# A one-core decoder layer on Trainium2: router heads every four items, gate products between the k steps, 34 more rows in the first half

## The reference, cut to what matters

```python
qv = (tb @ wq).reshape(n, PEER_HEADS, 2, PEER_HALF)
s = jnp.einsum('thcd,hckd->thck', qv, sub_keys).astype(jnp.float32)
s_top, i_top = lax.top_k(s, PEER_TOPK)
cand = (s_top[:, :, 0, :, None] + s_top[:, :, 1, None, :]).reshape(n, PEER_HEADS, -1)
...
best, pos = lax.top_k(cand, PEER_TOPK)
idx = jnp.take_along_axis(cand_idx, pos, axis=-1)
g = jax.nn.softmax(best, axis=-1).astype(tb.dtype)
u = expert_u[idx]
act = jax.nn.gelu(jnp.einsum('td,thkd->thk', tb, u))
v = expert_v[idx]
return jnp.einsum('thk,thkd->td', g * act, v)
```

## Time and profile before

| | us |
|---|---|
| median of 3 runs | 1953.18 (1946.73 to 1957.24) |
| the profiled execution | 1952.73, of which the span 1950.6 |
| mixer, in that span | 0 to 470 |
| U half (items 0 to 143) | 470 to 1243 |
| V half (items 144 to 271) | 1243 to 1818 |
| closing | 1818 to 1951 |

### The profile page before, as it was taken

One profiled execution on the slowest core, in us unless ns is written; L12 is line 12 of the kernel. 1 busy time (PEld: TensorE's weight loads), 2 busy tenths in 40 slices (PEclk: granted clock), 3 DMA queues, 4 the chain that ended last, 5 costly groups with the idle time before them and its releaser, 6 DMA issues.

```text
span 1950.6 us, 29824 instructions
## 1 busy us (share of the span) xinstructions
PE 1828.0 (94%) x11502; PEld 1756.7 (90%) x11502; DVE 1461.8 (75%) x2584; ACT 848.7 (44%) x1236; POOL 514.0 (26%) x415
## 2 busy tenths in 40 slices
PE   6999989998999999999999999699999999999694
PEld 5999977788999999999999999699999999999693
DVE  4736587556478778999999998588888878788524
ACT  4556672314333333347777776233233323323322
POOL 1200120000000002345444444344445444344000
PEclk9999989998999999999999999899999999999897
DMA  3222333114334447789999999999999999897111
GB/s 128 78 67 85 114 123 99 50 55 166 119 126 157 152 159 237 242 314 343 377 360 351 369 360 354 379 386 359 361 383 379 381 377 359 336 372 264 66 54 46
DMA packets 162616, 462.63 MB, mean 237 GB/s; under 512 B 16496, under 2 KB 74544, under 8 KB 160048
## 3 DMA queue, kind: packets, MB, share of 16 engines
q1 hardware_dynamic: 116400, 292.99, 41.5%
q0 software_dynamic: 46080, 167.79, 23.0%
HBM read 405.46 MB, written 55.27 MB: 236 GB/s over the span
## 4 chain that ended last, share of the span: by engine, by line
PE 69%; DVE 13%; DMA 11%; ACT 3%; issue 2%; SPq 1%; POOL 0%; DVEq 0%; ACTq 0%; POOLq 0%
PE PS L449 11%; DMA Rw<-vn 8%; PE PS L1416 8%; PE PS L1417 8%; PE PS L1418 8%; PE PS L1429 5%; PE PS L1430 5%; PE PS L1431 5%; PE PS L1405 5%; PE PS L1476 4%; PE PS L1898 3%; DVE Hl L1789 2%; PE PS L129 2%; ACT Rh L164 1%; DVE Rl L169 1%
## 5 line engine op out<-in xcount | busy, mean ns | idle before, releaser
L169 DVE TENSOR_TENSOR Rl<-Rw,Rh 128x1024 fp32r<-128x1024 f32 x272 | 332.1, 1222 | 171.2 <-ACT Rh L164 167.7
L164 ACT CAST Rh<-Rw 128x1024 fp32r<-128x1024 f32 x272 | 284.2, 1046 | 389.8 <-PE PS L1431 341.1
L1386 POOL DMA_INDIRECT ug<-un,idxU x160 | 239.2, 1495 | 579.6 <-DVE dots L1797 354.3
L1429 PE MATMUL PS<-Hh,Rh 128*128 128x384 f32 x1024 | 352.2, 344 | 37.1 <-DVE Hl L1789 36.9
L1416 PE MATMUL PS<-Xh,Rh 128*128 128x384 f32 x1024 | 353.9, 346 | 3.8 <-DVE Rl L169 2.7
L1430 PE MATMUL PS<-Hl,Rh 128*128 128x384 f32 x1024 | 349.1, 341 | 0.0
L1431 PE MATMUL PS<-Hh,Rl 128*128 128x384 f32 x1024 | 348.8, 341 | 0.0
L1417 PE MATMUL PS<-Xl,Rh 128*128 128x384 f32 x1024 | 345.0, 337 | 0.0
L1418 PE MATMUL PS<-Xh,Rl 128*128 128x384 f32 x1024 | 344.0, 336 | 0.0
L1386 POOL DMA_INDIRECT ug<-vn,idxU x160 | 232.2, 1451 | 280.2 <-DVE yacc L1802 218.6
L1429 PEld LDWEIGHTS PS<-Hh,Rh 128*128 128x128 f32 x1024 | 194.7, 190 | 46.5 <-issue 46.3
(11 more groups left out here) (378 smaller groups left out, 3074.6 us busy)
## 6 DMA issues: line engine op xcount, KB each, us to landing
Rw<-uw SPq DMA_DIRECT2D x144, 512.0 KB, 4.8
Rw<-vn SPq DMA_DIRECT2D x128, 512.0 KB, 7.9
Wr<-wm SPq DMA_DIRECT2D x51, 512.0 KB, 3.2
acts<-Ab SPq DMA_DIRECT2D x128, 192.0 KB, 5.4
gates<-stg SPq DMA_DIRECT2D x12, 2048.0 KB, 9.8
Gq<-gates SPq DMA_DIRECT2D x16, 1536.0 KB, 12.9
Aq<-acts SPq DMA_DIRECT2D x32, 768.0 KB, 10.3
w_ple_ring<-w_ple SPq DMA_DIRECT2D x8, 640.0 KB, 4.3
```

Source lines behind the costliest of these rows:

```text
L164: a.copy(self.Rh[:, q, :], self.Rw[:, q, :]).then_inc(self.S("rhi"), 1)
L169: v.tensor_tensor(self.Rl[:, q, :], self.Rw[:, q, :], self.Rh[:, q, :].bitcast(F32), ALU.subtract).then_inc(self.S("rlo"), 1)
L1386: p.indirect_dma_start(out=ug[:, r % 4, :], out_offset=None, in_=un if r < IDC else vn, in_offset=bass.IndirectOffsetOnAxis(ap=idxU[:, r % ...
L1429: pe.matmul(out, Rh[:, q, w], hh, start=(g == 0), stop=False)
```

## The change

- **Router.** Heads begin every four items (0, 4, 8, 12, then 24, 28, 32, 36), so that the items 0 to 15 and 24 to 39 are Q, U, Q, U. The six parts of `topk` stand in the iterations n + 5, 5, 6, 7, 7, 8. Decoding begins at the iterations 21 and 45; the lookups of block 0 and of the samples are both in the next iteration, then comes `softmax` with `idx`, then one lookup in each of the three iterations 24 to 26 and 48 to 50; `sx` is counted up at the end of the last.
- **Gates.** TURN is 51 (was 77), G0 is 55 (79), GEND is 131 (139). The products stand between the k steps of a U item: with one unit in an item one product after each second k step, with two units one after each. The wait for a unit's inputs and for `gev` is at its first product. `one_hot_act` runs two items ahead, as the one-hot matrices on DVE did and do.
- **Rows.** 30 rows after item 53, 156 after item 131, 180 after item 143; 140 are left to the V half. The GELU of the dot products (`sparse_act`) can therefore now fall in the U half.
- **Mixer.** DVE adds the squares of the channels 0 to 6 into `sqa` (`square_add`, six additions of 128x544), and PE sums twice instead of eight times, at the end. SP issues the load of `ce` for chunk 1 first, and it has a semaphore of its own.

```diff
-HEAD_AT = [0, 6, 12, 18, 34, 40, 46, 52]
-LOOK = [29, 63]
+HEAD_AT = [0, 4, 8, 12, 24, 28, 32, 36]
+LOOK = [21, 45]
...
             if n == 38:
+                sp.wait_ge(S("act_c"), 2 * NXC)
+                sp.wait_ge(S("cout_s"), 2 * NXC)
+                spread_e(1)
                 sp.wait_ge(S("mm"), OL0)
...
-            if n >= OS0 + 2:
-                d = n - OS0 - 2
-                if d == 0:
-                    pe.wait_ge(S("root"), 3)
-                sums(3, d, sq[:, d % 2, :])
-        for d in range(ND - 2, ND):
-            sums(3, d, sq[:, d % 2, :])
+        pe.wait_ge(S("root"), 3)
+        pe.wait_ge(S("sqa"), ND - 2)
+        for q in range(2):
+            m = pe.matmul(pair(3)[:, q, :], ones[:, :], sqa[:, q * HT:(q + 1) * HT], start=True, stop=False)
+        pe.wait_ge(S("sq_ready"), 4 * ND)
...
+        def square_add(d):
+            v.wait_ge(S("sq_ready"), 3 * ND + d + 1)
+            if d >= 2:
+                v.wait_ge(S("sqa"), d - 1)
+            v.tensor_tensor(sqa[:, :], sq[:, 0, :] if d == 1 else sqa[:, :], sq[:, d % 2, :], ALU.add
+                            ).then_inc(S("sqa"), 1)
...
-    TURN = 77
-    G0 = 79
-    GEND = 139
+    TURN = 51
+    G0 = 55
+    GEND = 131
...
-    ROWS = [(46, 0), (78, 36), (VI - 1, 146), (NALL - 5, 2 * IDC)]
+    ROWS = [(25, 0), (53, 30), (GEND, 156), (VI - 1, 180), (NALL - 5, 2 * IDC)]
...
+            turn = [(j, u) for j in units(m) for u in range(4)]
             for k in range(ND):
...
-            r.then_inc(S("wmm"), 1)
+                if k == ND - 1:
+                    r.then_inc(S("wmm"), 1)
+                for j, u in turn[k * len(turn) // ND:(k + 1) * len(turn) // ND]:
+                    gate_product(j, u)
...
+        def gate_product(j, u):
+            if u == 0:
+                pe.wait_ge(S("ga"), j + 1)
+                pe.wait_ge(S("gaa"), 2 * j + 2)
+                pe.wait_ge(S("gb"), j // 2 + 1)
+                need(pe, "gev", j - 1)
...
-            for j in units(n + 1):
+            for j in units(n + 2):
                 one_hot_act(j)
...
-            for part in range(6):
-                if head_at(n, 5 + part) is not None:
-                    topk(head_at(n, 5 + part), part)
+            for part, at in enumerate((5, 5, 6, 7, 7, 8)):
+                if head_at(n, at) is not None:
+                    topk(head_at(n, at), part)
...
-                if 1 <= step < 9 and step % 2 == 1:
-                    lookup(g, step // 2)
-                if step == 8:
+                if step == 1:
+                    lookup(g, 0)
                     lookup(g, NDB)
-                if step == 9:
+                if step == 2:
                     softmax(g)
+                if 3 <= step < 6:
+                    lookup(g, step - 2)
+                if step == 5:
+                    v.wait_ge(tc, ntc[0])
+                    v.sem_inc(S("sx"), 1)
```

More of the change, by code:

```diff
@@ L246, in mixer @@
     rstdB = at("rstdB", A6 + 2 * T * 4, [P, T])
+    sqa = at("sqa", A6 + T * 4, [P, T])
     yh = at("yh", A4, [P, ND, T], F32R)
@@ L625, in tensor @@
                     sums(2, k, sq8[:, k, :])
-            if n >= OS0 + 2:
-                d = n - OS0 - 2
-                if d == 0:
-                    pe.wait_ge(S("root"), 3)
-                sums(3, d, sq[:, d % 2, :])
-        for d in range(ND - 2, ND):
-            sums(3, d, sq[:, d % 2, :])
+        pe.wait_ge(S("root"), 3)
[3 more added lines that the diff above has]
+        pe.wait_ge(S("sq_ready"), 4 * ND)
+        for q in range(2):
+            m = pe.matmul(pair(3)[:, q, :], ones[:, :], sq[:, (ND - 1) % 2, q * HT:(q + 1) * HT], start=False,
+                          stop=True)
+        m.then_inc(S("sq_free"), ND)
     def scalar(a):
@@ L1231, in vector @@
                 ssd_add(n - OS0 - 1)
+                if n >= OS0 + 4:
+                    square_add(n - OS0 - 3)
             if n == NW - 1:
@@ L1234, in vector @@
                     ring.lo(v, m)
+        square_add(ND - 2)
         ring.lo(v, 3)
@@ L1466, in turns @@
                 m.then_inc(S("gtp"), 1)
-        def gate_unit(j):
-            pe.wait_ge(S("ga"), j + 1)
-            pe.wait_ge(S("gaa"), 2 * j + 2)
-            pe.wait_ge(S("gb"), j // 2 + 1)
-            need(pe, "gev", j - 1)
-            for u in range(4):
-                t = 4 * (j % 2) + u
-                out = PS[:, 2 + j % 2, u * PK:(u + 1) * PK]
-                m = pe.matmul(out, Boh[:, (j // 2) % 2, t, :], Aoh[:, j % 4, u, :], start=True, stop=True)
-            m.then_inc(S("gmm"), 1)
+        def gate_product(j, u):
[4 more added lines that the diff above has]
+                need(pe, "gev", j - 1)
+            t = 4 * (j % 2) + u
+            m = pe.matmul(PS[:, 2 + j % 2, u * PK:(u + 1) * PK], Boh[:, (j // 2) % 2, t, :], Aoh[:, j % 4, u, :],
+                          start=True, stop=True)
+            if u == 3:
+                m.then_inc(S("gmm"), 1)
         for n in range(NIT):
@@ L1489, in tensor @@
                 turns()
-            for j in units(n):
-                gate_unit(j)
         pe.wait_ge(S("glu"), PK)
@@ L1556, in h_hi, with sparse_act @@
             a.copy(Hh[:, i % 2, :, :], Aq[:, i % 3, :, :]).then_inc(S("hhi"), 1)
+        def sparse_act(n):
+            if rows_upto(n) >= IDC > rows_upto(n - 1):
+                a.wait_ge(S("sdt"), IDC)
+                a.activation(coef[:, :], dots[:, :], ACT.Gelu_apprx_tanh).then_inc(S("cf"), 1)
         def exps(g):
@@ L1589, in scalar @@
                 gate_out(j)
+            sparse_act(n)
             if n == NIT - 1:
@@ L1597, in scalar @@
                 h_hi(g // 4 + 1)
-            if rows_upto(n) >= IDC > rows_upto(n - 1):
-                a.wait_ge(S("sdt"), IDC)
-                a.activation(coef[:, :], dots[:, :], ACT.Gelu_apprx_tanh).then_inc(S("cf"), 1)
+            sparse_act(n)
     def vector(v):
```

12 lines of the change are left out of this document (4 added, 8 removed).

## The result

| | median, us | lowest to highest | ratio to before (95% interval) |
|---|---|---|---|
| before | 1954.6 | 1946.7 to 1957.2 | |
| after | 2012.0 | 2010.7 to 2016.5 | 1.0305 (1.0275 to 1.0335) |

What follows compares the result with a forecast made beforehand. PE was taken to set the pace, with waits in places and DMA and DVE nearly full. From 1952.7 us: mixer -5, gate waits +44, clock +14, turn +28, U half's end +5, V half -21 gave 2017 us; 8-in-10 range 1980 to 2044.

Steps and rivals of the forecast that it cites:

- The gate wait: Gate items: PE waits 2.3 us for ACT's bank copy behind each of 19 two-unit items, +44 us.
- the first rival: Gate items: k steps are not held, or ACT copies in time; the gate term goes, 1960 us, chance 0.08.
- The clock behind these waits: Gate items: lower PE clock costs 1.5 us more behind half of the 19 waits, +14 us (0 to +28).
- The turn: Behind item 51: PE waits for the last lookup after DVE's burst in iterations 41 to 50, net +28 us.
- its sign: Behind item 51: one long PE wait at the transposes, 17 us or more.
- The end of the U half: Items 132 to 144: DMA must carry 27.3 MB, 73 us against 50.5 of PE; net +5 us (-8 to +15).
- The V half: V items: 34 fewer rows relieve DMA and remove waits, -21 us (-27 to -12).
- The rival by which the rows give nothing: V half gains nothing, as waits on `Hl`, not bandwidth, set it: 2038 us, chance 0.08.
- The mixer: Before item 0: fewer ones matmuls and an earlier `ce` load against a longer end, sum -5.1 us (-6.5 to -3).
- the five groups of ones matmuls: Mixer: six groups of ones matmuls of 0.92 us were to leave PE's chain, -5.5 us.
- the earlier `ce`: Mixer: load issued some 3 us sooner, removing DVE's wait, -1.05 us.
- the end: Mixer's end: two DVE additions before PE's first sums, then a reciprocal waiting for ACT's root, +1.45 us.

Runs made afterwards that it cites:

- experiment 1: Changed kernel with the gate products behind an item's 24 k-step matmuls again instead of between them: 1962.5 us, ratio 1.0048 to the kernel before.
- experiment 2: Changed kernel with ACT copying the gate bank directly behind the copy of the item's output, products still between the k steps: 1976.6 us, ratio 1.0123.
- experiment 6: Changed kernel with the 34 rows back in the V half (row 126 at item 131, 146 at the end of the U half): 2022.4 us, ratio 1.0371.
- Experiment 7: Changed kernel with SP's wait for the stored gates and the first V-half loads six items later, at item 137: 2013.3 us, ratio 1.0320.
- Experiment 4: Kernel of experiment 1 with the turn behind item 57 instead of 51 and gates from item 61 instead of 55: 1951.9 us, ratio 0.9995.
- Experiment 5: Kernel before with only the rows' part of the change (180 rows, not 146, by the end of the U half; `sparse_act` there): 2004.5 us, ratio 1.0274.
- experiment 3: Kernel before with only the mixer's part of the change: 1945.9 us, ratio 0.9956.
- experiment 8: Kernel of experiment 1 with a looser timetable: second decoding at item 51, turn behind 61, gates in 65 to 129, fewer early rows: 1931.2 us, ratio 0.9894.

## Why the prediction was right, point by point

- **The gate wait** (+44, measured 44.1). The forecast had the place (the item behind one of two units), the count (19) and the size (2.3; such an item is 7.41 where its work is 5.09, so 2.32 longer). Experiments 1 and 2 show the cause: the wait goes with the place of the products, and shrinks with ACT's order. The k steps behind a waiting product waited with it, so the first rival fell: the product of item 68 started at 873.21 and the next k step at 873.63. That agrees with what the Trainium skill (TensorE: Matmul & The Clock Gate, Step-by-step: what each phase is for) says, that matmuls stay in program order.
- **The clock behind these waits** (+14, measured 4.6). This term was mis-sized. I took half of 19 from two V items; three of 19 (the items 68, 88 and 112, 8.9 to 9.0 us) had it, at 1.5 each. Two instances were no base for a share. The price of one was right. In the profiles of experiments 6 and 7, with the same 19 waits, it was three of 19 again.
- **The turn** (+28, measured +27.5). Part of it fell due earlier than forecast: 14 us were lost in the items 45 to 50 to the ring's low parts, and the turn's own wait was then 15.4, under the 17 or more that the prediction named as its sign. Experiment 4 shows that a later turn alone recovers 11 us; what stays behind is spent waiting for DVE.
- **The end of the U half** (+5, measured +7.1; 75.0 us for 50.5 of work, so 24.5 late where 22.5 was forecast). Experiment 7 moves the loads and not the time, which speaks for the amount of work, not SP's blocking; experiment 6 takes 4 rows of 24 and 30 earlier ones away and gains 7.9.
- **The V half** (-21, measured -24.3). Experiments 5 and 6 put and take the rows alone: -23.1 and +19.4. The rival by which the rows give nothing has fallen. The size is less sure than it looks: the three profiles with 146 rows before it have 575.0, 570.2 and 568.4 us for this half, and before's is the longest. That the relief was DMA's is argued: ACT waited 46.2 us for weights to land in this half of before and 6.4 in after's, but the rows also took 41 us of DVE's work with them. The Trainium skill (DMA: Bandwidth & Descriptors, Measured) gives 425 GB/s for a long stream. Over this half the mixed stream here moved 352 GB/s before and 335 after.
- **The mixer** (-5, measured +0.3 in the profile). The term failed in that profile. It had four parts: the five groups of ones matmuls gave -4.4; the earlier `ce` -1.15, of which 0.4 was lost again at the next chunk; the end cost +3.1 and not +1.45, as the eight last matmuls ran at 0.46 instead of 0.23 us each behind PE's idle time; and +1.55 was the clock behind an unchanged wait. The rest, +0.7, is there from the first loads on. Over all profiles the mixer gives -1.9, and over the runs of experiment 3 the kernel gains 7.7.

That the sum came within 5 us is partly luck, as errors cancelled: the clock's 9 and the V half's 3 too much stood against the mixer's 5 and the end's 2 too little.

What the prediction hardly asked is what the 34 rows cost in the U half: it checked DVE's time for the items and nothing else there. In after they looked free, since PE's waits had lengthened the gates' stretch to 458 us (a DMA share of 0.88, DVE 364 of 458 busy). Experiment 5 shows that they cost 73 in the timetable of before, 13 of them through `sparse_act`. They still fit in the 410 us of experiment 1, where the 96 units and 126 rows have 77 items and not 61.

## What to carry to other kernels

Before instructions are moved forward in a queue, list for each resource that they take who frees it and at which place of *its* queue: here the matmuls were moved by 3 us against an ACT that freed the bank fourth in its iteration, and each product of 0.2 us that was due too early cost 2.3 us. Put the release first in the other engine's iteration, or leave the consumer late. A wait of one engine for another is also a place in a queue: `sparse_act` held up everything behind it once its row came late. A burst on an engine that is nearly full was not hidden by moving one who waits for it (11 of 33 us came back); with less work in it and more items around it (experiment 8) it was gone.
